# A hybrid decoder trunk on one core: the decay-level scores issued between the halves of the next projection

## The reference

```
h = rmsnorm(x, attn_norm[l])
(hq, hf, hi, hg, mq, mk, mv, mi, mf, mo, fq, fk, fv, ff) = split(h @ w_in[l])
o_hg = hgrn2_mixer(hq, hf, hi, hg, ...)     # 4 heads of 64, a decay for each channel
o_ml = mlstm_mixer(mq, mk, mv, mi, mf, mo, ...)
o_fx = fox_mixer(fq, fk, fv, ff, ...)       # 8 heads, causal softmax with a forget gate
x = x + concat(o_hg, o_ml, o_fx) @ w_out[l]
```

```
scores[t, s] = sum_d q[t, d] * k[s, d] * exp(b[t, d] - b[s, d])
```

## Time and profile before

| | before |
|---|---|
| time, median of 3 runs | 1571.19 us (1570.28 to 1573.03) |
| profiled execution | 1573.09 us, its span 1571.3 us |
| PE busy over the span | 1480.6 us (94%) |
| DVE, ACT, POOL busy | 1166.0, 972.8, 92.7 us (74%, 62%, 6%) |
| mean granted TensorE clock | 0.972 of full speed |

### The profile page before, as it was taken

The page is one execution under the profiler, slowest core; times in us unless marked ns, Lnnn a source line. Parts: engine busy times, 40 slices in busy tenths (PEclk is TensorE's granted clock), DMA queues, the critical chain, the costliest instruction groups (busy, mean ns, idle before and its releaser), DMA issues.

```text
span 1571.3 us, 21095 instructions
## 1 busy us (share of the span) xinstructions
PE 1480.6 (94%) x8033; PEld 1258.3 (80%) x8033; DVE 1166.0 (74%) x921; ACT 972.8 (62%) x863; POOL 92.7 (6%) x103
## 2 busy tenths in 40 slices
PE   7989799997998969999999999999999999999993
PEld 6987499997988748888888888888888888888882
DVE  4883445454576347888888888888888889889884
ACT  6454244443646226777777777777777777777772
POOL 4221000000031121000000000000000000000001
PEclk9999899999899989999999999999999999999997
DMA  8431586534333167999999999999999999999983
GB/s 260 162 108 55 177 319 214 188 117 151 108 108 108 55 218 273 391 376 370 394 373 374 394 375 371 394 380 370 394 385 363 394 373 376 394 386 361 394 329 107
DMA packets 211785, 449.19 MB, mean 286 GB/s; under 512 B 12884, under 2 KB 37016, under 8 KB 211736
## 3 DMA queue, kind: packets, MB, share of 16 engines
q1 hardware_dynamic: 210584, 444.31, 77.9%
q0 software_dynamic: 1152, 4.19, 0.8%
HBM read 433.80 MB, written 14.68 MB: 285 GB/s over the span
## 4 chain that ended last, share of the span: by engine, by line
PE 88%; DVE 5%; ACT 4%; issue 1%; DMA 1%; POOL 0%; DVEq 0%; POOLq 0%; ACTq 0%; SPq 0%
PE bank L1369 26%; PE bank L1371 26%; PE bank L1370 26%; PE bank L1593 2%; PE bank L1580 2%; PE bank L1677 2%; ACT winh L711 1%; PE bank L1494 1%; DVE QD L993 1%; PE bank L1421 1%; ACT XN L679 1%; DVE low L1221 1%; DVE winl L961 0%; DVE SC L1002 0%; PE bank L1378 0%
## 5 line engine op out<-in xcount | busy, mean ns | idle before, releaser
L1221 DVE TENSOR_TENSOR low<-raw,high 128x2048 fp32r<-128x2048 f32 x336 | 768.8, 2297 | 112.2 <-ACT high L878 112.2
L878 ACT CAST high<-raw 128x2048 fp32r<-128x2048 f32 x336 | 644.0, 1917 | 178.1 <-PE bank L1371 178.1
L1369 PE MATMUL bank<-high,xeh 128*128 128x512 f32 x896 | 353.5, 395 | 0.0
L1371 PE MATMUL bank<-high,xel 128*128 128x512 f32 x896 | 349.5, 390 | 0.0
L1370 PE MATMUL bank<-low,xeh 128*128 128x512 f32 x896 | 348.8, 389 | 0.0
L1371 PEld LDWEIGHTS bank<-high,xel 128*128 128x128 f32 x896 | 168.2, 188 | 35.8
L1370 PEld LDWEIGHTS bank<-low,xeh 128*128 128x128 f32 x896 | 168.4, 188 | 33.7
L1369 PEld LDWEIGHTS bank<-high,xeh 128*128 128x128 f32 x896 | 168.3, 188 | 33.5
L1369 PE MATMUL bank<-high,hdh 128*128 128x512 f32 x448 | 175.0, 391 | 0.0
L1371 PE MATMUL bank<-high,hdl 128*128 128x512 f32 x448 | 174.4, 389 | 0.0
L1370 PE MATMUL bank<-low,hdh 128*128 128x512 f32 x448 | 174.4, 389 | 0.0
(11 more groups left out here) (288 smaller groups left out, 1967.7 us busy)
## 6 DMA issues: line engine op xcount, KB each, us to landing
raw<-in_moe_w_gate_dram SPq DMA_DIRECT2D x112, 1024.0 KB, 7.6
raw<-in_moe_w_up_dram SPq DMA_DIRECT2D x112, 1024.0 KB, 8.0
raw<-in_moe_w_down_dram SPq DMA_DIRECT2D x112, 1024.0 KB, 7.6
ring<-in_w_in_dram SPq DMA_DIRECT2D x10, 2048.0 KB
dring<-in_dense_w_gate_dram SPq DMA_DIRECT2D x5, 2048.0 KB
dring<-in_dense_w_up_dram SPq DMA_DIRECT2D x5, 2048.0 KB
dring<-in_dense_w_down_dram SPq DMA_DIRECT2D x5, 2048.0 KB
ring<-in_w_in_dram SPq DMA_DIRECT2D x8, 1024.0 KB
```

The lines of the kernel that those rows point to most:

```text
L878: act.copy(high[:, q % SPLIT, :], raw[:, q % RAW, :]).then_inc(s_hi, 1)
L1221: dve.tensor_tensor(low[:, q % SPLIT, :], raw[:, q % RAW, :], high[:, q % SPLIT, :].bitcast(F32), ALU.subtract).then_inc(s_lo, 1)
L1369: pe.matmul(o, xh, wh, start=first, stop=False)
L1371: return pe.matmul(o, xl, wh, start=False, stop=last)
```

## The change

`project` takes a function and calls it between its two runs of matmuls. In step k, for k from 1 to 9, that function is level(k - 1). The call of level(k) at the end of step k is gone. Nothing is added or taken away on any engine: 3366 rows stand in PE's list before and after, and the lists of DVE, ACT, POOL and SP are the same.

```
-            def project(l, i):
+            def project(l, i, between=None):
...
                         else:
                             ins = three(o, hTh[:, k, v], hTl[:, k, v], wh[:, k, :], wl[:, k, :], k == 0, k == KD - 1)
+                    if f == 0 and between is not None:
+                        between()
                 ins.then_inc(s_pp, 1)
...
-                    project(l, k + 2)
+                    project(l, k + 2, (lambda: level(l, k - 1)) if 1 <= k <= LEVELS else None)
...
-                    if k < LEVELS:
-                        level(l, k)
```

## The result

The kernel got faster, by about half of the 8.5 us that were forecast. In ten runs of each the median went from 1572.90 us to 1569.21, a ratio of 0.9976 with a 95% interval of 0.9967 to 0.9985. A second comparison on another occasion (5 runs against 9) gave 1573.24 and 1566.91, 0.9961 with an interval of 0.9947 to 0.9975. Over all 15 runs the mean is 1568.2, some 5 us under the mean of before. The first three runs of before, 1571.19, lay low: over all its 50 runs in these comparisons the median is 1573.0.

The account below looks back on a forecast made before the run. TensorE, 88% of the chain, was taken as the bound, with its waits for DVE. Waits 4.7 plus clock 3.8 gave 8.5 us: 1562.7 on the median (1564.6 profiled), range 1560.5 to 1567.5.

Parts of the forecast that it names:

- the clock: Three slow projections, one in the first layer and two in the second, return to full TensorE rate: 3.8 us gained.
- the fall behind the wait of 3.4 us: Second layer, projection 4: half clock after PE's wait for QD goes as that wait shrinks to 1.8; 1.5 us.
- The two behind step 3: Slow projections 6 of both layers, after four-row matmuls and level 3, go when level 3 moves; 1.0 and 1.3 us.
- slow clock in other projections: Sign that the forecast is wrong: half clock appearing in projections other than those expected; no size given.
- 4.7 us without the clock: Gain from PE's waits alone over both layers: 1.85 us in the first, 2.85 in the second.
- projection 4: Its start waits for DVE's low weights: new 0.7 us cost in first layer; second layer's wait shrinks from 3.4 to 1.8.
- the gain at CT: Level 7's 0.8 us gain is lost again, with 0.3 more, as the first attention scores wait 1.1 for CT.
- the busy falls stay: Rival: four-row matmuls still slow the clock in step 3, only the long wait's fall goes; 6.2 us gain, 1565.0, chance 0.20.
- as many falls come as now: Rival: new waits bring other clock falls, leaving a gain of 4.7 us, 1566.5; chance 0.12.
- DVE as the bound: Rival: convolution steps take DVE 7.4 us against PE's 7.1; gain 3.1 us or less, about 1568.5; chance 0.11.
- the closed loop: Rival: levels waiting mid-projection delay its end and the next copy, 14 waits in all; slower, 1574.9 at 0.6 each; chance 0.05.
- The idle rule: Rate halves after PE idles, so only the long wait's fall would go; gives the 1565.0 of that rival, chance 0.20.

Follow-up runs that it names:

- the filled kernel: Changed kernel with ten extra 256-column matmuls, results unused, in front of each layer's first attn_turn; measured 1567.22 us, 0.9962 of before.
- level 8 back: Changed kernel with level 8 returned to the end of its step, in front of the first attn_turn; alone it measured 1566.78 us, 0.9965 of before.
- the kernel before with the pairs: Kernel before the change, its four-row matmuls split two and two over the ends of the projections of steps 3 and 4; measured 1576.55 us, 1.0021 of before.

## Why the prediction was wrong

**The step that failed is the clock.** I priced it at 3.8 us, from three slow projections of one trace, on the ground that the change took level 3 away from the four-row matmuls and shortened the long wait. One of the three parts holds: the fall behind the wait of 3.4 us came in all 4 second layers in the old order and in none of 10 with the wait of 1.8. The two behind step 3 did not go as a pair (9 of 15 layers against 4 of 5). The piece of four-row matmuls itself is what the runs point to, since in two pairs it never brought one. And I gave new falls no price. They came at the first turn, in 12 of 15 layers with the levels moved and the turn and the scores left at the ends of their steps (the filled kernel aside), against 2 of 7 in the old order. Why is open: the longer wait that level 8 left is not enough to explain it, since with level 8 back the clock still fell in 4 of 6. My sign of being wrong, slow clock in other projections, came with them.

The count behind the price was one trace. Taken in pairs of traces, before has 4 and 5 falls in its mixers and after 4 and 3. A fall costs 1.5 us (level 1 to level 2 of the second layer took 8.61 us in place of 7.14), and my 1.0 and 1.3 were too small too, since the half clock had begun ahead of the projections that I measured. One in the second trace of before cost 0.7 at its own place, since the wait for SC behind it went away, but at the first turn PE then waited 0.8 longer:

```profile
499.41 0.66 PE L1461 MATMUL bank<-ident,XN 128*128 128x128 f32 x4 [1.96 <-DVE XN L1024]
```

Summed over the mixers, falls cost 6.7 us on the mean before and 5.1 after. The clock gave 1.6, not 3.8, and that is a difference of one fall between two traces each, which the draw alone can make.

**The waits were placed rightly and came out a little smaller.** The next term of the sum, 4.7 us without the clock, was too large by 1.5. Every wait that should go went, and every new one stands where the text had it: 0.62 and 1.7 at projection 4 (0.7 and 1.8), 1.06 for CT (1.1), nothing at level 6, and 0.3 more in front of the second half of the first turn. With falls taken out the first layer went from 107.9 to 106.9 us and the second from 110.1 to 107.9: 3.2 us in place of 4.7. The parts that the traces show: level 8 costs 0.8 a layer and not 0.65, as its return showed; the stretch from level 0 to level 1 takes 8.0 us against 7.14 for an undisturbed step, so the low weights of projection 4 cost 0.85 and not 0.7; and from level 2 to level 3 it takes 9.38 us, where the old order had 9.15, so a return from small matmuls to a projection in the middle of a step costs 0.2 that had no line in the sum. The same stretch of the second layer's projection 4 came out 0.1 over the 1.8. Together that is some 1.0 of the 1.5; the rest stays open.

**That the gain at CT is lost again** was right and is the largest lesson of the sum. To the first attention scores the first layer had 3.1 us and the second 4.2 (falls out). At the output projection 1.0 and 2.2 were left. The levels behind the whole projection showed it again: 1.7 us more ahead of the attention, and by the estimate above half of it at the end.

**The rivals.** That the busy falls stay is what happened for the two, and its price of 6.2 us of gain left out the new falls and the 1.5. That as many falls come as now, 4.7, is nearest to the mean over all runs, 5. DVE as the bound, and the closed loop, did not come. The idle rule of the Trainium skill (TensorE: Matmul & The Clock Gate, the HAM clock gate) has the fall behind the wait of 3.4 us on its side, and the one behind step 3 against it, where PE was busy throughout. At the first turn PE was idle, but with the levels moved it was so in two pieces of 0.7 to 1.5 us, in all but two of the layers, and the runs don't say whether these pieces count together.

**The range.** It was worked on a median of three runs that lay 1.7 us under that of ten, and its upper end took no account of how far a median of few runs can be off when each execution draws its own falls at 1.5 us apiece.

## What to carry to other kernels

Where an engine in program order waits for a short chain, issuing the waiting piece half a step later can be worth its waits, and the long piece needn't be split for it: behind the whole of it the piece did at least as well in the traces here. But move everything on the path: as long as the attention's own waits stood at the ends of the steps, most of the first layer's gain at the levels and half of the second's was given back to them, and moving them the same way was worth some 15 us, three times the change, with about 6 of it in falls of the clock that did not come. And falls of TensorE's clock in one trace are in part a draw: count them over several traces before giving one a price, and ask where new light stretches arise.

## What the runs showed of the hardware

The clock fell with PE busy without a gap: 2 us of matmuls on four rows stood ahead of a fall to 1.2 GHz in 13 of 20 layers, and pieces of 1 us in none of 8. With them in one piece it also held in both layers of the kernel with the attention in the middle, which I can't explain.

The same product QD takes DVE 0.68 or 1.78 us. In most steps POOL had begun its product KDk while DVE was still at the low weights in front of QD:

```profile
53.37 2.20 POOL L628 TENSOR_TENSOR KDk<-HK,DX 128x512 f32<-128x512 f32 x1 [4.98 <-ACT DX L795]
...
86.82 3.59 POOL L628 TENSOR_TENSOR KDk<-HK,DX 128x512 f32<-128x512 f32 x1 [4.93 <-ACT DX L795]
```

The first goes with the QD of 1.78 us at 54.35, the second with that of 0.68 us at 87.96. That fits the exclusive lock on the port pair of DVE and GpSimd that the Trainium skill describes (SBUF — State Buffer, Who interferes with whom), in that the loser waits for a whole instruction. Which of the two goes first is not explained. Where KDk had begun, an idle gap of DVE ahead of the low weights always went with the long QD, 84 times in these traces, but QD was long 44 times without a gap too. What parts the cases better is by how much KDk's start lies ahead of QD's: by 0.67 to 1.05 us QD was long in 127 of 127 cases, and by 1.14 us or more, with KDk still running, it was short in 63 of 63. Two cases with 0.29 us went one each way. In the kernel before with the pairs a gap of 0.77 us on DVE came with a QD that was 1.1 us longer.
